# Modulation blocks moved out of the state-space stage, setup reordered, query rotation interleaved

## Time and profile before

| | us |
|---|---|
| median of 3 runs (lowest, highest) | 1248.6 (1240.9, 1249.3) |
| the profiled execution, its own time | 1246.66 |
| span of the profiled execution | 1245.0 |
| PE busy / DVE / ACT / POOL in the span | 1112.8 / 829.0 / 564.4 / 260.9 |

### The profile page before, as it was taken

One profiled execution on the slowest core, in us unless ns is written; L12 is line 12 of the kernel. 1 busy time (PEld: TensorE's weight loads), 2 busy tenths in 40 slices (PEclk: granted clock), 3 DMA queues, 4 the chain that ended last, 5 costly groups with the idle time before them and its releaser, 6 DMA issues.

```text
span 1245.0 us, 19186 instructions
## 1 busy us (share of the span) xinstructions
PE 1112.8 (89%) x6852; PEld 734.5 (59%) x6852; DVE 829.0 (67%) x1309; ACT 564.4 (45%) x1145; POOL 260.9 (21%) x384
## 2 busy tenths in 40 slices
PE   3599999989859999999699987899998699999995
PEld 0365556555536666666467665545666366666663
DVE  3689887998676777843654356665454767777444
ACT  2411121212566666654462405664445566666542
POOL 1175554672001121100100020002430012121000
PEclk7789998999879999999899976979999899999998
DMA  8859877656313334344412520004894214432341
GB/s 351 325 185 409 339 295 267 243 200 227 133 69 128 143 136 141 126 149 161 160 69 87 189 82 1 1 1 134 282 297 180 107 70 166 171 136 94 140 153 43
DMA packets 52530, 205.01 MB, mean 165 GB/s; under 512 B 7251, under 2 KB 36051, under 8 KB 41811
## 3 DMA queue, kind: packets, MB, share of 16 engines
q1 hardware_dynamic: 49362, 195.40, 43.2%
q0 software_dynamic: 3072, 8.39, 2.2%
HBM read 199.39 MB, written 4.38 MB: 164 GB/s over the span
## 4 chain that ended last, share of the span: by engine, by line
PE 76%; DVE 10%; ACT 4%; DMA 3%; issue 3%; SPq 3%; DVEq 0%; POOL 0%; ACTq 0%; POOLq 0%
PE PS L472 16%; PE PS L471 15%; PE PS L475 14%; PE PS L611 8%; PE PS L484 4%; DVE space L1357 4%; PE PS L839 3%; DVE wk_sb L1357 2%; PE PS L640 2%; PE PS L810 2%; PE PS L495 2%; PE PS L758 2%; PE PS L589 1%; DVE rinv L1361 1%; SPq L372 1%
## 5 line engine op out<-in xcount | busy, mean ns | idle before, releaser
L471 PE MATMUL PS<-space_rounded 128*128 128x320 f32 x1344 | 566.4, 421 | 32.8 <-DVE space L1357 23.9
L472 PE MATMUL PS<-space_rounded,lo 128*128 128x320 bf16 x1344 | 428.3, 319 | 0.0
L475 PE MATMUL PS<-space,ring 128*128 128x320 bf16 x1344 | 403.3, 300 | 0.0
L1357 DVE TENSOR_TENSOR lo<-ring,space_rounded 128x1024 bf16<-128x1024 f32 (+1 forms) x172 | 205.8, 1200 | 226.1 <-ACT space_rounded L930 224.4
L471 PEld LDWEIGHTS PS<-space_rounded 128*128 128x128 f32 x1344 | 255.9, 190 | 100.4 <-DVE space L1357 28.9
L930 ACT ACTIVATE space_rounded<-ring 128x1024 fp32r<-128x1024 f32 (+1 forms) x172 | 176.7, 1032 | 225.7 <-PE PS L472 221.8
L472 PEld LDWEIGHTS PS<-space_rounded,lo 128*128 128x128 bf16 x1344 | 129.8, 97 | 125.0 <-issue 2.8
L475 PEld LDWEIGHTS PS<-space,ring 128*128 128x128 bf16 x1344 | 135.7, 101 | 0.0
L611 PE MATMUL PS<-space 128*128 128x256 f32 x512 | 116.8, 387 | 0.0
L611 PEld LDWEIGHTS PS<-space 128*128 128x128 f32 x512 | 97.5, 193 | 28.8 <-issue 15.9
L1357 DVE TENSOR_TENSOR space<-space 128x256 f32<-128x256 f32 (+9 forms) x217 | 85.0, 409 | 22.4 <-ACT space L997 16.0
(11 more groups left out here) (206 smaller groups left out, 1438.8 us busy)
## 6 DMA issues: line engine op xcount, KB each, us to landing
ring<-w_mod SPq DMA_DIRECT2D x24, 2048.0 KB, 9.0
ring<-w_up SPq DMA_DIRECT2D x22, 2048.0 KB, 8.0
ring<-w_down SPq DMA_DIRECT2D x16, 1408.0 KB, 6.0
space<-pool_cmp SPq DMA_DIRECT2D x128, 128.0 KB, 2.8
ring<-w_mod_kv SPq DMA_DIRECT2D x4, 2048.0 KB, 10.6
ring<-w_kv SPq DMA_DIRECT2D x3, 2048.0 KB, 9.3
ring<-w_glu SPq DMA_DIRECT2D x2, 2048.0 KB, 10.5
ring<-w_q SPq DMA_DIRECT2D x2, 2048.0 KB, 12.4
```

What stands on the lines that cost most here:

```text
L471: pe.matmul(out, wr[:, p % SPLIT, at:at + P], xr[:, k, :], start=start, stop=False)
L472: mm = pe.matmul(out, lo[:, p % SPLIT, at:at + P], xh[:, k, :], start=False, stop=False)
L475: return pe.matmul(out, w, xl[:, k, :], start=False, stop=stop)
L1357: return dve.tensor_tensor(out, a, b, op)
```

## The change

- Modulation: each of the 16 units makes one chunk (4 to 19). Chunks 20 and 21 are made around the outputs of the last unit, 22 behind the last GLU tile and ahead of the norm's sum, 23 behind that sum, 24 behind the last tile of the first down product, 25 and 26 ahead of and behind `sums(4)`, 27 inside the K/V product behind its sixth tile. In the table of chunks 22 and 23 stand between `glu1` and `up0_0`; 24, 25 and 26 between `down0_7` and `kv0`; 27 behind `kv0`. Blocks 5 and 6 are copied to other places in SBUF.
- Setup: SP issues the parameters and constants ahead of the first chunks; PE makes `sums(0)` and chunk 3 ahead of the transposes, and the bias product for the keys ahead of unit 0.
- Query: the rotations are interleaved with the tiles of Q; the compressed scores of the samples are 32 matmuls of 32 weight columns, one for each sample and head, in place of 16 of 128; the output of the K/V rows is issued behind chunk `k0` and no longer ahead of `q0`.
- In units 1 to 7 SP issues the unit's chunk behind its 8 pages (before: in units 2 to 7).

The diff, cut to its core:

```diff
-        mod_of_unit = []
-        nxt = NMOD0
-        for u in range(units):
-            n = 2 if u < 28 - NMOD0 - units else 1
-            mod_of_unit.append(list(range(nxt, nxt + n)))
-            nxt += n
+        mod_of_unit = [[NMOD0 + u] for u in range(units)]
...
+        mod_chunks(range(NMOD0, 22))
         for j in range(2):
             add_chunk(f"glu{j}", whole(dram["w_glu"][j]), "glu_mm", 4 * j + 4)
+        mod_chunks((22, 23))
...
         ffn_chunks(0)
+        mod_chunks((24, 25, 26))
         for j in range(3):
             add_chunk(f"kv{j}", whole(dram["w_kv"][j]), "kv_mm", 4 * j + 4)
+            if j == 0:
+                mod_chunks((27,))
...
-            chunk(stream[0][0])
-            sp.dma_start(pages[:, :], dram["page_table"]).then_inc(S("pages_in"), 16)
             sp.dma_start(lam, dram["lam"].rearrange("p (i s) -> p i s", s=ST)).then_inc(S("params_in"), 16)
...
             sp.dma_start(consts[:, :], dram["consts"]).then_inc(S("params_in"), 16)
+            sp.dma_start(pages[:, :], dram["page_table"]).then_inc(S("pages_in"), 16)
+            for n in range(RING):
+                chunk(stream[n][0])
...
-                if name == "gate":
+                if name == "k0":
                     sp.wait_ge(S("roped"), 4)
                     sp.wait_ge(S("kv_ev"), 12)
                     sp.dma_start(dram["out_kv"], KV).then_inc(S("out_kv"), 16)
...
                         mm.then_inc(S(f"{tag}_mm"), 1)
+                        if beside is not None and m >= 1:
+                            beside(m - 1)
                         m += 1
+                if ahead_of_sum is not None:
+                    modulation(ahead_of_sum)
                 if norm is not None:
...
             for j in range(NMOD0 - 1):
                 modulation(j)
+            sums(0)
+            modulation(NMOD0 - 1)
             pe.wait_ge(S("bx_done"), 4)
...
-            sums(0)
-            modulation(NMOD0 - 1)
+            page_bias(0)
             pe.wait_ge(S("bt_ev"), 4)
...
-                for j in mod_of_unit[u][1:]:
-                    modulation(j)
+            modulation(20)
             compressed(units - 1)
             outputs_of(units - 1)
+            modulation(21)
 
-            dense("glu", ["glu0", "glu1"], KT, gb, 4, (0, 1, 2, 3), "glu_ev", ("g_lo", 0), norm=1)
+            dense("glu", ["glu0", "glu1"], KT, gb, 4, (0, 1, 2, 3), "glu_ev", ("g_lo", 0), norm=1, ahead_of_sum=22)
+            modulation(23)
             sums(2)
             ffn(0)
 
+            modulation(25)
             sums(4)
-            dense("kv", ["kv0", "kv1", "kv2"], KT, hb_kv, 4, (0, 1, 2, 3), "kv_ev", split_of(4))
+            modulation(26)
...
+            dense("kv", ["kv0", "kv1", "kv2"], KT, hb_kv, 4, (0, 1, 2, 3), "kv_ev", split_of(4), beside=last_modulation)
...
-            dense("q", ["q0", "q1"], KT, hb_kv, 4, (0, 1, 2, 3), "q_ev", split_of(5))
-            for i in range(4, 12):
-                pe.wait_ge(S("q_ev"), i - 3)
-                rotated(i, Qp[:, i - 4, :])
+            dense("q", ["q0", "q1"], KT, hb_kv, 4, (0, 1, 2, 3), "q_ev", split_of(5), beside=rotated_query)
+            rotated_query(KT - 1)
...
-                for hh in range(2):
-                    mm = pe.matmul(PS[:, 7, NC * b:NC * b + NC], QBp[:, hh, b, :], kcT[:, b, hh, :], start=(hh == 0), stop=(hh == 1))
+                for hd in range(KVH):
+                    mm = pe.matmul(PS[32 * hd:32 * hd + 32, 7, NC * b:NC * b + NC], QBp[:, hd, b, :], kcT[:, b, hd // 2, :], start=True, stop=True)
```

More of the change, by code:

```diff
@@ L276, in build_step, with mod_chunks @@
         blocks_of_unit = [[j // 4 for j in js if j % 4 == 3] for js in mod_of_unit]
-        for u in range(units):
-            for j in mod_of_unit[u]:
+        def mod_chunks(js):
+            for j in js:
                 add_chunk(f"mod{j}", whole(mod_src[j]), "mod_mm", j + 1)
+        mod_chunks(range(NMOD0, 22))
         for j in range(2):
             add_chunk(f"glu{j}", whole(dram["w_glu"][j]), "glu_mm", 4 * j + 4)
+        mod_chunks((22, 23))
         def ffn_chunks(l):
@@ L407, in _ @@
             sp.dma_start(w1, dram["cmp_w1"][0].rearrange("p (l n) -> p l n", n=P)).then_inc(S("w1_in"), 16)
+            for j in mod_of_unit[0]:
+                chunk(f"mod{j}")
             sp.wait_ge(S("pages_in"), 16)
@@ L424, in _ @@
                                  dram["pool_cmp"][e][page(NPG * b + j)]).then_inc(S(f"xt{u % 2}_in"), 16)
-                if 2 <= u < DB:
+                if 1 <= u < DB:
                     for j in mod_of_unit[u]:
                         chunk(f"mod{j}")
-            for j in range(2):
-                chunk(f"glu{j}")
+            for name in ("mod20", "mod21", "glu0", "glu1"):
+                chunk(name)
             sp.dma_start(prefix, dram["prefix"][0].rearrange("p (j a b r) -> p j a b r", a=2, b=DB, r=2)).then_inc(S("prefix_in"), 16)
@@ L434, in _ @@
             sp.dma_start(dram["out_ssm"], FS.rearrange("p s e b -> p (s e b)")).then_inc(S("out_ssm"), 16)
-            first_after = place["up0_0"]
+            first_after = place["mod22"]
             for n in range(first_after, len(stream)):
@@ L501, in h_ready, with dense @@
                 pe.wait_ge(S("hs"), nth_mod[r])
-            def dense(tag, chunks, kt, src, per, banks, ev, ready, norm=None):
+            def dense(tag, chunks, kt, src, per, banks, ev, ready, norm=None, beside=None, ahead_of_sum=None):
                 m = 0
@@ L517, in dense @@
                                 mm.then_inc(S(f"{tag}_mm"), 1)
+                    for i in range(2):
+                        if beside is not None:
+                            beside(i)
                 for name in chunks:
@@ L558, in ffn @@
                     mm.then_inc(S(f"up{l}_mm"), 1)
-                dense(f"down{l}", [f"down{l}_{j}" for j in range(8)], FT, U, 1, down_banks, f"down{l}_ev", (f"u_lo{l}", 0), norm=(3, 8)[l])
+                dense(f"down{l}", [f"down{l}_{j}" for j in range(8)], FT, U, 1, down_banks, f"down{l}_ev", (f"u_lo{l}", 0), norm=(3, 8)[l],
+                      ahead_of_sum=(24, None)[l])
             pe.wait_ge(S("silc"), 1)
@@ L571, in _, with page_bias @@
                     mm.then_inc(S("bt_mm"), 1)
-            sums(0)
-            modulation(NMOD0 - 1)
+            def page_bias(e):
+                pe.wait_ge(S("w1_in"), 16 * (e + 1))
+                if e == 1:
+                    pe.wait_ge(S("hid_sum"), 2 * DB)
+                for l in range(16):
+                    mm = pe.matmul(PS[:, 6, 500:501], w1[:, l, :], pe_[:, e, l:l + 1], start=(l == 0), stop=(l == 15))
+                mm.then_inc(S("pb_mm"), 1)
+            page_bias(0)
             pe.wait_ge(S("bt_ev"), 4)
@@ L595, in hidden @@
                 if u % DB == 0:
[L596 removed]
                     if e == 1:
[L598 to L601 removed]
+                        page_bias(1)
                     pe.wait_ge(S("pb_ev"), e + 1)
@@ L990, in gate_of, with page_bias @@
                 act.activation(SG[:, j % 3, :], CV[:, j % 3, 1, :], ACT.Silu).then_inc(S(f"sg{l}"), 1)
+            def page_bias(e):
+                act.wait_ge(S("pb_mm"), e + 1)
+                act.activation(cmp_bias[:, e:e + 1], PS[:, 6, 500:501], ACT.Identity, bias=V["cmp_b1"][:, e:e + 1]).then_inc(S("pb_ev"), 1)
+                act.wait_ge(S("pb_ev"), e + 1)
             act.wait_ge(S("eps"), 1)
@@ L1451, in ffn @@
                     low_parts(2)
+                    if l == 0 and j == 2:
+                        turned_modulation(5)
+                        gate_weights(48, g_post[:, 2])
                     s = j % 3
@@ L1653, in _ @@
             gate_weights(0, g_post[:, 0])
-            for i, tile in ((1, 24), (2, 48), (3, 72)):
-                norm_weights(tile, g_pre[:, i], g_post[:, i])
+            norm_weights(24, g_pre[:, 1], g_post[:, 1])
+            norm_weights(48, g_pre[:, 2], None)
             norm_weights(96, V["norm_kv"], None)
```

61 lines of the change are left out of this document (40 added, 21 removed).

## The result

The changed kernel takes 1258.7 us in the median of 20 runs (1249.7 to 1267.3), the kernel before 1246.1 in 20 (1240.3 to 1257.1). The ratio is 1.0084, 95% interval 1.0058 to 1.0110, some 10.5 us; the two medians by themselves lie 12.5 us (1.0%) apart. The change made the kernel a little slower. The forecast was 1251, range 1238 to 1264, and most of the chance on "within 1%".

What follows compares the result with a forecast made beforehand. PE is three quarters of the chain of waits, but DVE's period limits the units. Terms -9.1 - 6.3 - 2.0 + 1.8 + 13.1 + 17.2 + 1.9 - 12.3 = +4.3 on 1246.7 gave 1251 us, range 1238 to 1264.

Steps and rivals of the forecast that it cites:

- `up0_0`: End of the GLU: weight issued only after the last GLU product, ACT's pieces wait for it; +13.1 us, bounds 11 and 17.
- `kv0`: End of the first down product: weight issued late, ACT must make two pieces before copying tile 7; +17.2 us, bounds 14 and 19.
- Rival A: Late weights at the ends of GLU and down product not needed until the next stage: 1220 us; chance 0.12.
- Rival B: Modulation chunks come late in units 1 to 7: slower, 1270 us if they take 13 us to land; chance 0.13.
- Rival C: The start gives only its lower bound: 1255 us, or 1260 with a half-clock score product; chance 0.15.
- Setup: Start of the kernel: DVE enters unit 0 at 56.2 us, before at 65.29; -9.1 us, bounds 5 and 11.
- The signs: Profile after: ACT idle about 8 us at the GLU's end, 12 after the first down product; PE over 10 at both.
- Query: From Q to the samples' scores: earlier q0, rotations among Q's tiles, shorter scores (-3.1); together -12.3 us, bounds -8 and -15.
- Units 0 to 2: First two units: 28.3 us with DVE alone as limit, for 30.3 before; -2.0 us.
- Units 2 to 8: One chunk less on PE, period falls to DVE's 14.25 us from 15.3; -6.3 us.
- Units 8 to 15: Later units, with one chunk each already before: no term in the sum, 0.
- Chunks 20 and 27: Chunk 20 ahead of the last unit's compression, +1.8 us; chunk 27 inside K/V, where PE has no gap, +1.9.

Runs made afterwards that it cites:

- filler: TensorE products nobody reads: in units 1 to 7 of the changed kernel, ratio 1.0133; ahead of the second prompt head, on setup and query together, 0.9790.
- modulation alone: The changed kernel with its setup order, rotations and K/V write put back as before, the samples' scores kept in 32-column form: 1275.3 us, ratio 1.0235.
- setup and query together: The kernel before with the change's setup and query parts, all modulation chunks left in the units: 1225.3 us, ratio 0.9844.

## Why the prediction was right, and where it was not

- **The order of things was right.** Two late weights, `up0_0` and `kv0`, eat what the start and the query bring. Rival A (late weights hurt little) falls with the earlier trace rows read against the rows after. Rival B falls, since nothing in the units waits for w_mod. Rival C falls: the start gave its full term.
- **Setup**, -9.1: -8.8 by the ratio alone. Right, by the mechanism it named: the inputs were waited for, then DVE, then POOL's tables. A slip in it did no harm: it added the inputs' landing to 29.5 us and then took 29.2; DVE came to them at 28.28.
- **`up0_0`**, +13.1: 13.1 by the table. The landing of 7.97 against 8.2 and the work behind it came out as summed; in the seven other traces with this change it is 7.77 to 8.48. The fit of the Trainium skill (DMA: Bandwidth & Descriptors, "Anatomy of one DMA") gives an estimated 6.8, at least 1 us too short by all these; the page made it for transfers that GpSimd issues, and these are SyncE's. **`kv0`**, +17.2: 18.5. The landing was 12.08 us after its issue (11.1 to 12.5 in the other traces), for the 10.5 that were taken; the upper bound of 19 was the nearer one. SP issued two more transfers, of 0.75 MB together, right behind `kv0`; `up0_1`, also the second of a pair but without such followers, landed in 10.96. The signs named waits of ACT of about 8 and 12 us; they were 16.25 and 21.52, as ACT had come to the two pieces early, while PE's waits of 13.28 and 16.17 were the "over 10" forecast.
- **Query**, -12.3: -11.5 by the ratio. But the scores fell by 6 us where 3.1 stood. The Trainium skill (TensorEngine Tiling (Array Packing), "Theoretical Speedup") gives up to four times for 32 columns; 7.09 to 1.91 at the same clock is 3.7 times, so the rule was nearer than the row of a small matmul used for the estimate. The rest, 1.91 to 1.09, is full clock for half, which came with the rotations' new place. What took the surplus back is not settled: PE now waits 3.57 us for the importance sums, where it waited 0.20 before, which gives 1.2 us back ahead of the second prompt head (12.5 us from the end of the scores to it, for 11.3), and the rest is within what the attention varies by from one execution to the next.
- **Units 0 to 2**, -2.0: 36.2 us for 38.2, right.
- **Units 2 to 8**, -6.3: this term was too large. The period fell to 14.6 and not to 14.25, -4.3. The forecast took DVE's pace from units 9 to 15 of before. There DVE is busy for 13.24 us of a period and idle for 1.01; in units 2 to 8 of the changed kernel it is busy for 13.72 and idle for 0.87. So the missing 0.34 us lies in DVE's own instructions, the same in number and shape, and not in waits for PE. Their length goes with what POOL does beside them: in all 14 traces the 85 scans that overlap a 128x512 product of POOL take 3.58 to 3.92 us, the other 139 take 2.82 to 2.93. The change shifts DVE's work in time against POOL's tables, and with it which instructions meet. The window of the earlier trace rows is itself one of the slow kind; POOL's mean busy time in units 9 to 15 was 8.6 us, not 12.13. PE's half clock behind its waits is the obvious rival for the missing time, and DVE's idle time does not bear it out.
- **Units 8 to 15**, 0: 2.3 us longer in the profiled execution. Unit 8 has 1.1 of it (22.1 us for 21.0, 22.3 to 22.8 in the other traces of the change without filler), with a scan of 3.58 for 2.83. The other 1.2 are this execution's alone: units 9 to 15 take 86.7 us in it, 85.5 before, and 85.2 to 85.5 in those other traces.
- **Chunks 20 and 27**, +1.8 and +1.9: the stretch from unit 15 to the GLU's first tile grew by 0.7; K/V and Q grew by 3.8 in modulation alone, chunk 27 and something of DVE's block 6, not separated.
- **The sum.** The modulation's terms made +22.6 with the scores' -3.1 in them, and +29 was measured; setup and query together -19 for -21.4. So +10 came out instead of +4, inside the range. The profiled execution shows +4.3 because up to the samples' scores it has +6.4, and its attention took 230.6 us for 233.6, at a mean granted clock of 0.93 for 0.90. The range held because it was wide enough for terms that were together 6 us off; that the profiled execution hit the centre was luck.

## What to carry to other kernels

In a ring of buffers the place of a chunk in the table is its issue time. Moving another chunk into the table ahead of a weight delays that weight, and the damage is done where some engine asks for it *first*, here a look-ahead piece that stood ahead of the current stage's last tiles. Move such a piece behind the work that others wait for before moving transfers; here that took about 27 us off. And where an engine is not the bound of a stage (PE in the units, once one chunk is out), taking more work out of it is worth only what the other engine's period leaves.

When PE waits twice in a row for DVE or ACT, look at the duration of the products behind the wait. If they are twice as long as their like elsewhere, products that nobody reads in the wait can pay: 5 us here in the attention, nothing in the units, where they made PE the limit again.

## What was not expected of the hardware

- 32 products of 32 output columns by 63 streamed took 1.09 us at full clock and 1.91 at half, in place of 7.09 at half for 16 of 128 columns.
- DVE's scan of 1280 columns took 3.58 to 3.92 us where it overlapped a 128x512 product of POOL, and 2.82 to 2.93 elsewhere; POOL's product took 3.67 us there for 1.28. Moving one engine's work against the other's changes a stage's length without any change in the work.
- The attention, the same code but for the filler, took 222.8 to 241.5 us in the traces, and the granted clock of its first 120 us goes the same way: 1.00, 0.91, 1.00 in the first three stretches of 20 us of the shortest, 0.62, 0.69, 1.00 and then 0.83, 0.76, 0.82 in the longest. What makes one execution better than another there was not settled. In single profiles this hides or doubles a gain of 3 to 9 us ahead of it.
